# The last six mixing weight loads in four raw slots, and two expert loads moved ahead

## The reference

```
h = RMSNorm(x);  p = h @ W_in                 # one projection for all mixers and the merge gates
A = chunked gMLP gating;  B = top-64 sparse attention;  C = gated short convolution
mix = sum_i sigmoid(gate_i) * (branch_i @ W_proj_i);  x = x + mix @ W_out
x = x + HierMoE(RMSNorm(x))                   # 32 experts: gate, up (1024 x 512), down (512 x 1024), top 2 of one group
```

## Time and profile before

| what | value |
|---|---|
| median of 3 runs | 1439.09 us (1438.97 to 1439.96) |
| the profiled execution | 1437.3 us |
| its span | 1435.6 us |
| mean granted TensorE clock | 0.992 of full speed |
| TensorE (matmul) busy | 1385.5 us, 97% |
| VectorE, ScalarE busy | 559.2 us and 361.2 us |
| moved by DMA | 490.19 MB, mean 341 GB/s |

### The profile page before, as it was taken

The page is one execution under the profiler, slowest core; times in us unless marked ns, Lnnn a source line. Parts: engine busy times, 40 slices in busy tenths (PEclk is TensorE's granted clock), DMA queues, the critical chain, the costliest instruction groups (busy, mean ns, idle before and its releaser), DMA issues.

```text
span 1435.6 us, 17698 instructions
## 1 busy us (share of the span) xinstructions
PE 1385.5 (97%) x7295; PEld 833.4 (58%) x7295; DVE 559.2 (39%) x882; ACT 361.2 (25%) x532; POOL 6.3 (0%) x36
## 2 busy tenths in 40 slices
PE   5999999999999999999889999999999999999996
PEld 5899888644444444444378988885444444444442
DVE  6686655432221221221267757355222122122213
ACT  5554442311111111111155444422111111111111
POOL 0000000000000000000000000000000000000000
PEclk9999999999999999999989999999999999999999
DMA  8655767899999999999946457578999999999995
GB/s 282 195 189 177 252 203 278 347 422 421 421 421 421 421 420 421 421 422 421 405 138 220 153 200 265 204 317 346 422 421 420 420 421 422 421 421 421 420 421 226
DMA packets 101125, 490.19 MB, mean 341 GB/s; under 512 B 8717, under 2 KB 12085, under 8 KB 51893
## 3 DMA queue, kind: packets, MB, share of 16 engines
q1 hardware_dynamic: 99940, 488.72, 85.4%
q10 hardware_dynamic: 1104, 0.34, 0.1%
HBM read 487.98 MB, written 1.05 MB: 341 GB/s over the span
## 4 chain that ended last, share of the span: by engine, by line
PE 89%; DVE 7%; issue 2%; ACT 1%; DMA 0%; DVEq 0%; SPq 0%; ACTq 0%
PE psB L1644 31%; PE psC L1655 16%; PE psA L1392 13%; PE psB L1392 12%; PE psA L1633 8%; PE psA L1670 3%; PE psA L1671 2%; DVE parts L944 2%; PE psD L1697 1%; DVE score_work L1039 1%; DVE top L1038 1%; ACT parts L740 1%; PE psC L1608 1%; DVE score_work L1034 0%; DMA rows<-in_conv_w_dram 0%
## 5 line engine op out<-in xcount | busy, mean ns | idle before, releaser
L1644 PE MATMUL psB<-slot,uT 128*64 128x512 f32 x2048 | 458.8, 595 | 0.0
L1644 PEld LDWEIGHTS psB<-slot,uT 128*64 128x64 f32 x2048 | 141.2, 137 | 268.4 <-issue 265.6
L1655 PE MATMUL psC<-slot,ybT_plain 128*64 128x512 f32 x1024 | 227.2, 595 | 2.8 <-ACT ybT_plain L855 2.7
L944 DVE TENSOR_TENSOR parts<-slot,parts 128x2048 fp32r<-128x2048 f32 (+1 forms) x80 | 177.4, 2248 | 70.3 <-ACT parts L740 70.0
L740 ACT ACTIVATE parts<-slot 128x2048 fp32r<-128x2048 f32 (+1 forms) x80 | 147.9, 1879 | 92.8 <-PE psA L1392 50.1
L1655 PEld LDWEIGHTS psC<-slot,ybT_plain 128*64 128x64 f32 x1024 | 70.9, 137 | 135.1 <-issue 128.2
L1268 DVE TENSOR_TENSOR x<-x,psA 128x1024 f32<-128x1024 f32 x62 | 75.7, 1221 | 186.3 <-PE psA L1671 186.3
L1392 PE MATMUL psB<-parts,hT_parts 128*128 128x512 f32 x448 | 138.9, 391 | 0.2
L1633 PEld LDWEIGHTS psA<-sel_mem,xn 128*128 128x128 f32 x1024 | 119.2, 192 | 27.0 <-issue 25.7
L839 ACT ACTIVATE rel_parts<-psC 128x512 fp32r<-128x512 f32 x62 | 37.1, 598 | 385.5 <-PE psC L1655 259.3
L1633 PE MATMUL psA<-sel_mem,xn 128*128 128x128 f32 x1024 | 127.4, 278 | 2.5 <-DVE sel_mem L1227 2.5
(11 more groups left out here) (302 smaller groups left out, 1179.2 us busy)
## 6 DMA issues: line engine op xcount, KB each, us to landing
slot<-in_expert_w_gate_dram SPq DMA_DIRECT2D x128, 1024.0 KB, 21.7
slot<-in_expert_w_up_dram SPq DMA_DIRECT2D x128, 1024.0 KB, 23.2
slot<-in_expert_w_down_dram SPq DMA_DIRECT2D x128, 1024.0 KB, 24.3
slot<-in_w_in_dram SPq DMA_DIRECT2D x56, 1024.0 KB, 5.1
slot<-in_w_out_dram SPq DMA_DIRECT2D x8, 1024.0 KB, 5.1
slot<-in_w_proj_b_dram SPq DMA_DIRECT2D x4, 1024.0 KB, 5.0
slot<-in_w_proj_c_dram SPq DMA_DIRECT2D x4, 1024.0 KB, 4.9
slot<-in_w_proj_a_dram SPq DMA_DIRECT2D x4, 1024.0 KB, 5.0
```

The source lines that it names most:

```text
L944: v.tensor_tensor(low_part, mix_slot(i), high_part, ALU.subtract).then_inc(low_dve, 1)
L1644: ins = te.matmul(psB[j * BLK:(j + 1) * BLK, o, :], xT[:, 4 * half + c, j * BLK:(j + 1) * BLK], w[:, c, :], start=half == 0 and c == 0, st ...
L1655: ins = te.matmul(psC[j * BLK:(j + 1) * BLK, n, :], hidT[:, 2 * k + c, j * BLK:(j + 1) * BLK], w[:, c, n * 512:(n + 1) * 512], start=k == ...
```

## The change

Six raw slots stay for uses 0 to 33. Uses 34 to 39 get the four raw slots 14, 15, 16, 17, 14, 15. So the load of use i among these waits for the last use of the same slot: use 34 waits for use 30 instead of 28, 35 for 31 instead of 29, 36 for 32 instead of 30, 37 for 33 instead of 31, 38 for 34 instead of 32, and 39 for 35 instead of 33. Slots 12 and 13 are last used by uses 28 and 29; their expert loads are issued right behind the load of use 36 and ahead of that of use 37, and the two `load_raw` calls behind the mixing loads are gone. All other loads keep their order, and the high slots and the work of the other engines are the same.

```diff
+    LATE_USES, LATE_RAWS = 6, 4
+    GIVEN_BACK = RAWS - LATE_RAWS
+
     def raw_slot(i):
+        late = i - (MIX_SLOTS - LATE_USES)
+        if late >= 0:
+            return RAW0 + GIVEN_BACK + late % LATE_RAWS
         return RAW0 + (i + RAWS - MIX_SLOTS % RAWS) % RAWS
+
+    def raw_use_ahead(i):
+        return [k for k in range(i) if raw_slot(k) == raw_slot(i)][-1]
...
                 def load_mix(i):
 
                     if i >= RAWS:
-                        wait_used(sp, l, i - RAWS)
+                        wait_used(sp, l, raw_use_ahead(i))
...
                 for i in range(MIX_SLOTS):
 
                     load_mix(i)
+                    if i == MIX_SLOTS - LATE_USES + 2:
+                        for s in range(RAW0, RAW0 + GIVEN_BACK):
+                            wait_used(sp, l, [k for k in range(MIX_SLOTS) if raw_slot(k) == s][-1])
+                            load_main(s)
...
-                load_raw(MIX_SLOTS - 6)
                 sp.wait_ge(merged_done, l * 2 + 2)
                 load_main(GATES_AT)
                 load_main(GATES_AT + 1)
-                load_raw(MIX_SLOTS - 5)
                 sp.wait_ge(merged_ps, l * 2 + 2)
                 load_main(MERGED_AT)
```

## The result

| | before | after |
|---|---|---|
| median | 1439.15 us (1438.97 to 1439.96, 4 runs) | 1454.5 us (1453.03 to 1455.4, 4 runs) |
| ratio | | 1.0102, 95% interval 1.0087 to 1.0118 |
| span of the profiled execution | 1435.6 us | 1451.3 us |

The change makes the kernel 15.3 us slower; 1453.1 were forecast. The profiled execution after is the one of 1453.03 us, 15.7 above that of before. In the kernel after, the lines of the functions are 11 higher: L1392 is now L1403, L740 is L751, L749 is L760, L944 is L955, L1151 is L1162, L1139 is L1150, L1552 is L1563. In the kernels of the experiments the lines can be up to three higher again.

The account below looks back on a forecast made before the run. TensorE was taken to bound the kernel, with 89% of the chain. A stall of 5.3 us and a clock loss of 1.7 in each of two layers, 14.0 us, turn 1439.1 into 1453.1 us; range 1447.5 to 1456.5.

Parts of the forecast that it names:

- The earlier loads bring nothing: Experts: two loads issued earlier gain 0, as the next load waits for pair 0's first stage; bounds 0.3 us either way.
- Steps 1 to 3: Mixing: later loads 34 and 35 stay hidden, load 36 lands at 218.3, the expert loads at 220.8 and 223.3 us.
- Step 4: Mixing: load 37 waits for use 33 and queues behind the expert loads, so high 37 runs 7.3 us later.
- Step 5: Ahead of use 36: the product it needs moves by 7.3 us, margin 2.0, so TensorE stalls 5.3 us per layer.
- Step 6: After use 36: loads 38 and 39 stay hidden, 2.3 us to spare; 1 to 2 us if that cover fails.
- The clock: Use 36 behind the stall: clock falls to half speed for 3.4 us, losing 1.7 us per layer, 3.4 in all.
- The sum: Whole kernel: stall and clock in two layers, 2 x (5.3 + 1.7) = 14.0 us slower.
- Rival B: Ahead of use 36: stall with the clock unharmed, 1439.1 + 10.6 = 1449.7 us; chance 0.25.
- Rival C: Mixing: load 37 not held by expert loads, stall 3.1 us, too short for the clock, 1445.3 us; chance 0.07.
- D: Mixing: no stall, the raw slots' depth was slack all the way, 1439.1 us; chance 0.04.
- E: Experts: their DMA work sets each layer's end and 5.0 us is done ahead, so faster, 1429.1 us; chance 0.02.

Follow-up runs that it names:

- experiment 6: The reordered kernel: changed kernel, with merged_part(0) ahead of high 37 on ScalarE, use 34's product and sum ahead of low 37 on VectorE; 1439.62 us, ratio 1.0004.
- experiment 8: Kernel before, but the first expert load behind the 20 early ones waits for pair 0's second stage instead of its first; 1445.73 us, ratio 1.0048.
- experiment 1: Changed kernel with shared raw slots, but the two expert loads back behind the mixing loads; 1449.28 us, ratio 1.0071.
- experiment 2: Changed kernel, but the two expert loads issued right behind load 34 instead of load 36; 1447.68 us, ratio 1.0056.
- experiment 3: Kernel with shared slots and expert loads back behind the mixing loads, plus 12 pairs of dummy matmuls ahead of use 36 per layer; 1445.12 us, ratio 1.0046.
- experiment 5: Changed kernel with 20 pairs of dummy matmuls ahead of use 36, placed ahead of the wait for low 36; 1450.89 us, ratio 1.0087.
- experiment 4: Changed kernel with 20 pairs of dummy matmuls ahead of use 36, placed behind the wait for low 36; 1454.08 us, ratio 1.0115.

## Why the prediction was right

By its own steps:

- **The earlier loads bring nothing.** Shown: the reordered kernel has them and measures 1.0004. The reason given, the empty queue ahead of pair 0, is seen after (DMA share 0.00), and experiment 8 shows that the restart sets the end.
- **Steps 1 to 3.** Loads 34 and 35 landed 5.0 us after their issues behind uses 30 and 31. ScalarE waited for them (3.9 and 3.6 us, in time it had free), TensorE did not. The expert loads were issued right behind load 36.
- **Step 4, load 37.** 7.3 us after use 33 until high 37, forecast; 7.2 in layer 0 (227.41 - 220.22) and 7.4 in layer 1. The two terms were tested apart. The wait for use 33 with the landing alone makes a stall of 3.0 (experiments 1, 2 and 3); the two loads ahead make the other 2.2 to 2.5.
- **Step 5, the stall.** 5.3 us forecast, 5.2 and 5.5 measured, ended by the product L1162. That program order turns the late load into a stall is shown by experiment 6.
- **Step 6, loads 38 and 39.** Covered, as forecast: after use 36 TensorE has no gap up to the residual.
- **The clock.** 3.4 us forecast for both layers. Use 36 was 3.95 longer in the profile, 3.4 of it the clock's by experiment 5, whose medians give 3.0. The lower level lay on 3.4 us of work in layer 0, the length taken from the earlier trace rows, and on 4.0 in layer 1, where it had begun some 3 us ahead, within the stall. That the loss came out so close is partly luck: the lower level lasted some 7 us in layer 1, twice the length that the prediction took, and 3 of them cost nothing only because they fell in the stall. In experiment 2 a fall of 6.8 us lay mostly on use 36 and cost 2.9.
- **The sum.** 14.0 forecast, 14.65 in the two places, 15.3 by the medians.

Rival B (the clock unharmed, 1449.7) is close to what experiment 5 measured, 1450.9, so its price was right and its condition was not met. Rival C (load 37 not held by the loads ahead) fell by the 7.15 us. D fell, although a stall of zero was one slot away. E (the lead makes it faster) fell twice, by the slower kernel and by experiment 6. What the prediction had not seen is that the clock can fall behind shorter idle stretches as well: 3.0 us in experiment 2, 2.3 in experiment 8. It priced rival C without the clock, at 1445.3; the kernels with that stall measured 1449.3 and 1447.7, and with dummy matmuls in it 1445.1.

Open is in part why the first product of the kernel takes 7.33 us in some profiled executions and 9.0 to 9.6 in others, with the same kernel up to there. The granted clock reads 1.00 in both. But the pace of the slow one is that of the lower level: 9 matmuls in 2 us after, 16 before, and 9 as well in layer 1 before, where the same product runs at 0.50. First after, then the two of before:

```profile
20.00:22.00 2.00, 2.00 (x9) 2.00 (x9) 2.00 (x1) 1.72 (x1) 0.00 (x0) 1.00 1.05 388
```

```profile
20.00:22.00 2.00, 2.00 (x16) 2.00 (x15) 1.88 (x1) 1.89 (x2) 0.00 (x0) 1.00 1.04 384
728.00:730.00 2.00, 2.00 (x9) 2.00 (x9) 2.00 (x1) 1.72 (x1) 0.00 (x0) 0.50 0.00 0
```

So a lower clock that the record doesn't show at the start of the trace is the likely cause; it isn't shown.

## What to carry to other kernels

When a buffer is shared more tightly, compare the distance that is left, in time, with the time to landing plus what is ahead in the queue. Then follow the copy that waits for it in its engine's program order: what is late is not the load's own user but the first thing behind that copy. Moving data earlier is worth something only if the queue isn't empty in between. Here it was, so 2 MiB of lead per layer bought nothing. A stall of a few microseconds in dense matmuls can cost more than its length, here by a third, where the clock is low when the work begins again.

## What the runs showed of the hardware

- Loads of 1 MiB on one queue landed in the order of their issue and some 2.5 us apart: after, those issued at 214.8, 215.2, 215.8 and 220.2 us landed at 219.7, 222.2, 224.8 and 227.4. Load 37 took 7.1 to 8.5 us behind two expert loads (8 landings in 4 profiles: after and experiments 4, 5 and 6), alone 4.9 to 5.1.
- The granted clock stayed at 2.4 GHz through an idle stretch of 5.2 us and fell as the work began, at about 237.2 us, while it fell in mid-idle in the other layer, at about 950.6. Behind 3.0 us of idle it fell in one layer and not in the other of one execution (experiment 2), and behind 2.3 us it fell 1 us after the work had begun again (experiment 8).
- Twenty pairs of 128-column dummy matmuls, 4.5 us, in the stall kept the clock at 2.4 GHz in both layers, even where 2.1 us of idle followed them (layer 1 of experiment 5).
